# Four of sixteen low parts of a recurrence turn made by GpSimd instead of VectorE

## The chip, the cores and the metric

The program runs on one core of a Trainium2 chip (trn2). Its time is that of one launch on the device, in microseconds, from the first instruction to the last. The median of three runs of the kernel before is given, and one execution of it was profiled.

## The reference

Two layers of a hybrid block and one block of a second kind, for 256 tokens of width 2048 in float32. The part that matters here is the gated delta rule of each layer: 16 heads of width 128, chunks of 64 tokens.

```python
u = h @ w_in
qkv_a, beta_a, a_a, z_a, ... = split_cols(u, SPLIT_SIZES)
qkv_a = jax.nn.silu(causal_conv(qkv_a, conv_w))
q_a, k_a, v_a = ...                      # 16 heads of 128
q_a = l2norm(q_a) * (GDN_HEAD_DIM ** -0.5)
k_a = l2norm(k_a)
o_a = gated_delta_rule(q_a, k_a, v_a, g, beta)
...
# gated_delta_rule: l_mat = strict(k_beta @ k.T * decay), a_mat = l_mat + I
sol = lax.linalg.triangular_solve(a_mat, rhs, lower=True, unit_diagonal=True)
# per chunk: v_new = u - w @ state; o = q @ state + qk @ v_new
#            state = state * dec + k.T @ v_new
```

## The kernel before

**Products in three parts.** All weights and activations are float32, and each is used as a high part, rounded to the format `fp32r`, and a low part, the remainder. A product is high by high, high by low and low by high (L283, L284, L285 in `pe_half`). The weights stream from memory in slabs of 128 x 2048 into a ring of four, `raw`. A slab holds two half blocks of 128 x 1024. For each half block ScalarE makes the high part `Wh` by a copy (`act_cast`, L348), VectorE makes the low part `Wl = raw - Wh` (`dve_low`, L354), and TensorE then has 24 matmuls of 256 columns. `Wh` and `Wl` are rings of four half blocks, so the two engines work three to four half blocks ahead. Counters carry this: `landed` (a slab is in), `hi_ready`, `lo_ready`, `half_used` (TensorE is done with a half block). TensorE waits for `lo_ready` before a half block, and the queue that refills `raw` (SyncE) waits for `lo_ready` too.

**The recurrence loop.** For each layer the 16 heads are taken as 8 pairs. A turn has 16 half blocks (q, k, v and z of one pair of heads, 8 blocks of 128 columns). The first turn of a layer only projects (`fresh`), the last only computes the recurrence of the pair before (`chain`), and the seven turns between do both: they are the full turns, 14 in the program, in a hardware loop. Each engine has its own function for a turn: `pe_gdn`, `act_gdn`, `pool_gdn`, `dve_gdn`. In the last one, half block by half block, n = 0 to 15, stands what VectorE does: `before(n)`, the low part, `after(n)`, `front(n)`. The order on each engine is that of the code. In a full turn VectorE is one late: in step n it makes low part m = n - 1, and the last one after the loop. Low part m of a turn is for half block m + 4; cast m is ScalarE's copy for the same half block, and waits until TensorE has finished half block m.

**What stands around the low parts.** With `LEVEL = 2` and `SCAN = 8`, steps 2 to 7 invert the unit triangular matrix by levels: TensorE makes `Z`, VectorE masks it into `Zm` (L1324), TensorE makes `MZ` (L1104), VectorE writes it into `M` (L1355, `copy_predicated` from PSUM) and packs the next `t_of` by a reduce (L1359). In step 7 VectorE copies `Zm64` out of PSUM (L1316) and TensorE, in the middle of its half block 7, waits for it at L1109. Steps 8 to 12 are the scan over chunks. Beside it, `front` and the table `TAPS` spread the convolution of the next pair over the steps: each channel block has one `tensor_scalar` (L1306, tap 0) and three `scalar_tensor_tensor` (L1309, taps 1 to 3), all 128x256 from SBUF. In step 6 stand tap 3 of one block and taps 0 and 1 of the next, right before `Zm64`. In step 10 stand `vn` (L1333, from PSUM), low 9, the silu product of q and k (L1402, after ScalarE's tanh L1207) and taps 0 and 1 of block 4; in step 11 low 10 and taps 2 and 3; in step 12 the two `sq_lo` (L1428), the low parts of the squares of q and k. TensorE sums these squares with `ones_r` (L1131, L1132, called `ssq`) in its half block 12, after six of its eight tiles.

**GpSimd** makes the three decay matrices of the next pair: `e0`, `e1`, `e2` (L1285, 128x512, rows minus columns) and `E0`, `E1`, `E2` (L1287, plus a mask), with one element pauses (L1257) that carry waits: for the transfer `gb` ahead of `e0`, for TensorE's `Z64` ahead of `e1`, for `turn64` ahead of `odd` (L1281, which clears half of `Mm`), and for `o_second` (L1055) ahead of `e2`.

Of the kernel before, what the change touches and what calls it, by code (L numbers as in the profile page):

```python
# [18 lines left out]
F32 = mybir.dt.float32  # L19
F32R = mybir.dt.float32r  # L20
I32 = mybir.dt.int32
ALU = mybir.AluOpType
# [4 lines left out]
D = 2048  # L27
# [4 lines left out]
PAIRS = HEADS // 2  # L32
# [11 lines left out]
Q_PRE, Q_GDN, Q_END, Q_SWA, Q_OUT = 1, 2 * PAIRS, 8, 2 * KV, 4  # L44
Q_LAYER = Q_PRE + Q_GDN + Q_END + Q_SWA + Q_END + Q_OUT
# [78 lines left out]
def build_program(nc, places, x_t, c_t, pos, stream, ada, ple_w, ple_x, rg_w, rpb, consts, params, params2, out_t, until=None):  # L124
    ctx = ExitStack()
    with ctx:
        def sb(name, shape, dt=F32):
            return ctx.enter_context(nc.sbuf_tensor(name, shape, dt))

        def sem(name):  # L130
            return ctx.enter_context(nc.semaphore(name))
# [6 lines left out]
        raw = sb("raw", [P, 4, D])  # L138
        Wh = sb("Wh", [P, 4, D // 2], F32R)
        Wl = sb("Wl", [P, 4, D // 2], F32R)  # L140
# [20 lines left out]
        def const(name, a=0, b=None):  # L161
            at, n = CONST_AT[name]
            return C[:, at + a:at + (n if b is None else b)]
# [23 lines left out]
        raw_used = sem("raw_used")  # L187
        hi_ready = sem("hi_ready")
        lo_ready = sem("lo_ready")
        half_used = sem("half_used")  # L190
        tile_ready = sem("tile_ready")
        tile_taken = sem("tile_taken")
# [7 lines left out]
        def stage(name, seeded=()):  # L200
            stages.append(Steps(nc, ctx, name, places, seeded))
            return stages[-1]
# [16 lines left out]
        st_gdn = stage("gdn", seeded=("dve",))  # L219
        st_fr = stage("gdn_front")  # L220
# [129 lines left out]
        def dve_low(dve, q, sbk, k):  # L350

            n = 2 * sbk + 4 + k
            dve.wait_ge(hi_ready, q * 8 + n + 1)
            dve.tensor_tensor(Wl[:, n % 4, :], raw[:, (sbk + 2) % 4, k * (D // 2):(k + 1) * (D // 2)],  # L354
                              Wh[:, n % 4, :].bitcast(F32), ALU.subtract).then_inc(lo_ready, 1)

        def act_tile(act, q, sbk):

            act.wait_ge(half_used, q * 8 + (2 * sbk + 2))
# [623 lines left out]
        def u4(v):  # L983
            return v.rearrange("p (u c) -> p u c", u=4)

        def tok(a, c, half=None):

            if half is not None:
                return TOK[:, a, :].rearrange("p (c h t) -> p c h t", h=2, t=2)[:, bass.ds(c, 1), :, half].rearrange("p c h -> p (c h)").unsqueeze(2).to_broadcast([P, 2, P])
            return TOK[:, a, bass.ds(c * 4, 4)].unsqueeze(2).to_broadcast([P, 4, P])  # L990

        def mask4(name):
            return const(name).unsqueeze(1).to_broadcast([P, 4, P])
# [8 lines left out]
        def even(v, odd=0):  # L1002
            return v.rearrange("p u (n two) -> p u n two", two=2)[:, :, :, odd]
# [250 lines left out]
        def pool_gdn(pool, l, i, fresh, chain):  # L1254

            def pause(at=0):
                pool.tensor_tensor(SEC_X[0:1, at:at + 1], ident[0:1, 0:1], ident[0:1, 0:1], ALU.subtract)  # L1257

            S, F = st_gdn, st_fr
            if chain:  # L1260
                S.start("pool")
                r = l * PAIRS + (i - 1)
            if fresh:
                F.start("pool")
                f = l * PAIRS + i
                if not chain:
                    st_pre.wait(pool, "act", "tok_exp", l)
                    pool.tensor_tensor(Zz[:], mask4("ident"), mask4("ident"), ALU.subtract).then_inc(zz_clear, 1)
                F.wait(pool, "dma", "gb", f)
                pause()  # L1270
                rows = [gb[:, 0].rearrange("p h (t c) -> p (h t) c", c=P), gb[:, 1].rearrange("p h (t c) -> p (h t) c", c=P)]
                e = [u4(E[:, n, :]) for n in range(3)]
                for n, (a, b, m) in enumerate(((rows[0], tok(1, i), "m_low"), (tok(0, i), rows[1], "m_up"), (tok(0, i), rows[0], "m_upd"))):
                    if chain and n == 1:
                        S.wait(pool, "pe", "Z64", r)
                        pause()
                    if n == 2:
                        if chain:
                            S.wait(pool, "pe", "turn64", r)
                            pause(8)  # L1280
                        F.done(pool.tensor_tensor(even(Mm[:], 1), even(mask4("ident"), 1), even(mask4("ident"), 1), ALU.mult), "pool", "odd")  # L1281
                    if chain and n == 2:
                        S.wait(pool, "pe", "o_second", r)
                        pause()
                    F.done(pool.tensor_tensor(e[n], a, b, ALU.subtract), "pool", f"e{n}")  # L1285
                    F.wait(pool, "pool", f"e{n}", f)
                    F.done(pool.tensor_tensor(e[n], e[n], mask4(m), ALU.add), "pool", f"E{n}")  # L1287

        def dve_gdn(dve, l, i, fresh, chain):
            S, F, q = st_gdn, st_fr, l * Q_LAYER + Q_PRE + 2 * i  # L1290
# [21 lines left out]
            def before(n):  # L1312
                if n == LEVEL + LEVELS - 1:
                    S.wait(dve, "pe", "Z64", r)
                    dve.wait_ge(zz_clear, l + 1)
                    S.done(dve.tensor_copy(Zz[64:P, :, 0:64], B[0][64:P, 0:256].rearrange("p (u s) -> p u s", u=4)), "dve", "Zm64")  # L1316
                elif LEVEL <= n < LEVEL + PACKED:
                    s = 2 << (n - LEVEL)
                    S.wait(dve, "pe", f"Z{s}", r)
                    if s == 32:  # L1320
                        S.done(dve.tensor_tensor(Zq.rearrange("p (u c) -> p u c", u=4), B[0][:, 0:T].rearrange("p (u c) -> p u c", u=4),
                                                 of_unit.unsqueeze(2).to_broadcast([P, 4, 64]), ALU.mult), "dve", "Zm32")
                        return
                    S.done(dve.tensor_tensor(Zq.rearrange("p (u i c) -> p u i c", u=4, i=4), B[0][:, 0:T].rearrange("p (u i c) -> p u i c", u=4, i=4),  # L1324
                                             sib(n).rearrange("p (u c) -> p u c", u=4).unsqueeze(2).to_broadcast([P, 4, 4, 16]), ALU.mult), "dve", f"Zm{s}")
                if n == SCAN:
                    S.wait(dve, "pe", "WT", r)
                    S.done(dve.tensor_copy(WT[:], B[1][:, 0:2 * P].rearrange("p (h c) -> p h c", c=P)), "dve", "WT")
                if n == SCAN + 2:
                    S.wait(dve, "pe", "VS", r)  # L1330
                    S.wait(dve, "act", "U", r)
                    uu = U[:].rearrange("p (h t) c -> p h t c", t=2)[:, :, 1, :]
                    S.done(dve.tensor_tensor(uu, uu, B[2][:, 0:2 * P].rearrange("p (h c) -> p h c", c=P), ALU.subtract), "dve", "vn")  # L1333
# [84 lines left out]
            for n in range(16):  # L1418
                if chain:
                    before(n)  # L1420

                if fresh and n == (SCAN + 4 if chain else SCAN + 3):
                    for h in range(2):
                        if not chain:
                            F.done(dve.memset(SEC_X[0:1, 16 + h:17 + h], 0.0), "dve", f"sq_lo{h}")
                            continue
                        F.wait(dve, "act", f"sq{h}", f)
                        F.done(dve.tensor_tensor(sq_lo[h], tm2[:, 2 * h:2 * h + 2, :], sq_hi[h].bitcast(F32), ALU.subtract), "dve", f"sq_lo{h}")  # L1428
                if n or not chain:
                    late = 1 if chain else 0  # L1430
                    dve_low(dve, q + (n - late) // 8, (n - late) // 2 % 4, (n - late) % 2)
                if chain:
                    after(n)
                if fresh:
                    front(n)
# [1446 lines left out]
def build(scratch, nc, shapes, until=None):  # L2882

    places = {}
    for core in (scratch, nc):
        args = [core.dram_tensor(f"in_{n}", shape, dt, kind="ExternalInput").ap() for n, (shape, dt) in shapes.items()]
        args.append(core.dram_tensor("out_0", (P, KT, T), F32, kind="ExternalOutput").ap())
        build_program(core, places, *args, until=until)
# [12 lines left out]
```

## Time and profile before

| | |
|---|---|
| median of three runs | 3900.39 us (3900.19 to 3901.93) |
| span of the profiled execution | 3899.3 us |
| TensorE busy | 3753.7 us, 96% |
| VectorE busy | 2862.0 us, 73% |
| ScalarE busy | 1904.5 us, 49% |
| GpSimd busy | 186.2 us, 5% |
| low parts (L354) | 1124, mean 1235 ns |
| casts (L348) | 1124, mean 1047 ns |
| share of the chain that ended last | PE 83%, DVE 8%, ACT 4% |

In the profile PE is TensorE's matmuls, DVE VectorE, ACT ScalarE, POOL GpSimd. A busy share says which engine has little air, and the list of waits says whether another engine ever keeps it waiting. Matmuls are pipelined: one is shown as 0.28 us long, but the next starts 0.12 us later. A duration of VectorE or GpSimd is counted from its issue, so that the time in which it is held up by the other is inside it: two rows of the same line and shape with different durations are the thing to look for.

### The profile page before, as it was taken

What the parts mean: (1) busy time and instruction counts of PE and PEld (TensorE: products, weight loads), DVE (VectorE), ACT (ScalarE), POOL (GpSimd) and SP (SyncE); (2) the same over time, 40 slices, a digit from 0 to 9 for tenths busy, and PEclk for the clock granted to TensorE, in tenths of its full rate; (3) what the DMA queues carried; (4) which work ended last, traced back from release to release, by engine and by line L of the source; (5) the groups of instructions that cost most, each with busy time, mean ns of one, the idle gap of its engine ahead of it and who ended that gap; (6) DMA issues with size and microseconds to landing.
All of it is one profiled execution on the core that took longest, in us unless ns stands there. A gap on an engine that the chain in (4) does not pass through costs nothing.

```text
span 3899.3 us, 70287 instructions
## 1 busy us (share of the span) xinstructions
PE 3753.7 (96%) x27254; PEld 3506.0 (90%) x27254; DVE 2862.0 (73%) x3924; ACT 1904.5 (49%) x2898; POOL 186.2 (5%) x188
## 2 busy tenths in 40 slices
PE   1999999999999999999999999999999999999998
PEld 1999999899988999999989998999987888989888
DVE  8788887867779778888686776665676666666676
ACT  1556565335544355555534554454665433334365
POOL 0111111000000012121000000000000000000000
PEclk8999999999999999999999999999999999999999
DMA  9543443864468843434486444444534455555543
GB/s 397 180 146 139 143 141 139 305 228 166 152 242 315 284 147 141 149 136 151 143 316 216 158 153 178 182 164 174 189 121 150 173 184 184 184 184 184 182 143 129
DMA packets 138699, 720.49 MB, mean 185 GB/s; under 512 B 37696, under 2 KB 38144, under 8 KB 62336
## 3 DMA queue, kind: packets, MB, share of 16 engines
q1 hardware_dynamic: 111456, 631.31, 45.1%
q10 hardware_dynamic: 27040, 86.32, 6.5%
q8 instruction: 146, 2.39, 0.2%
q14 instruction: 57, 0.47, 0.0%
HBM read 711.22 MB, written 2.16 MB: 183 GB/s over the span
## 4 chain that ended last, share of the span: by engine, by line
PE 83%; DVE 8%; ACT 4%; issue 3%; DMA 2%; DVEq 0%; ACTq 0%; SPq 0%
PE bank L300 16%; PE bank L283 13%; PE bank L285 13%; PE bank L284 13%; PE bank L301 8%; PE bank L322 3%; PE bank L2408 2%; PE bank L2410 2%; PE bank L2409 2%; ACT Wh L348 2%; PE bank L326 2%; DMA raw<-in_ada 1%; DVE Wl L354 1%; PE bank L1075 1%; DVE gm_more L1306 1%
## 5 line engine op out<-in xcount | busy, mean ns | idle before, releaser
L348 ACT CAST Wh<-raw 128x1024 fp32r<-128x1024 f32 x1124 | 1167.5, 1047 | 1617.8 <-PE bank L285 917.4
L354 DVE TENSOR_TENSOR Wl<-raw,Wh 128x1024 fp32r<-128x1024 f32 x1124 | 1380.9, 1235 | 701.4 <-ACT Wh L348 698.4
L283 PE MATMUL bank<-H,Wh 128*128 128x256 f32 x4928 | 1446.6, 294 | 2.0 <-DVE Wl L354 1.2
L284 PE MATMUL bank<-H,Wh 128*128 128x256 f32 x4928 | 1393.8, 283 | 0.0
L285 PE MATMUL bank<-H,Wl 128*128 128x256 f32 x4928 | 1393.1, 283 | 0.0
L283 PEld LDWEIGHTS bank<-H,Wh 128*128 128x128 f32 x4928 | 942.4, 191 | 26.1 <-issue 13.6
L284 PEld LDWEIGHTS bank<-H,Wh 128*128 128x128 f32 x4928 | 943.0, 191 | 8.1 <-issue 4.8
L285 PEld LDWEIGHTS bank<-H,Wl 128*128 128x128 f32 x4928 | 942.0, 191 | 0.0
L300 PE MATMUL bank<-H,Wh 128*128 128x512 f32 x1792 | 632.8, 397 | 6.3 <-DVE WS L341 6.2
L301 PE MATMUL bank<-H,Wl 128*128 128x256 f32 x1792 | 502.3, 280 | 0.0
L300 PEld LDWEIGHTS bank<-H,Wh 128*128 128x128 f32 x1792 | 337.4, 188 | 90.2 <-DVE Wl L354 5.3
L301 PEld LDWEIGHTS bank<-H,Wl 128*128 128x128 f32 x1792 | 339.3, 189 | 0.0
L300 PE MATMUL bank<-O,Wh 128*128 128x512 f32 x896 | 321.6, 401 | 6.2 <-DVE both L341 6.2
L301 PE MATMUL bank<-O,Wl 128*128 128x256 f32 x896 | 252.5, 282 | 0.0
L300 PEld LDWEIGHTS bank<-O,Wh 128*128 128x128 f32 x896 | 170.0, 190 | 50.8 <-DVE Wl L354 6.5
L2408 PE MATMUL bank<-O,Wh 128*128 128x256 f32 x704 | 199.9, 284 | 2.8 <-DVE WS L341 2.8
L2409 PE MATMUL bank<-O,Wh 128*128 128x256 f32 x704 | 199.1, 283 | 0.0
L2410 PE MATMUL bank<-O,Wl 128*128 128x256 f32 x704 | 199.1, 283 | 0.0
L301 PEld LDWEIGHTS bank<-O,Wl 128*128 128x128 f32 x896 | 170.9, 191 | 0.0
L326 PE MATMUL bank<-H,Wl 128*128 128x256 f32 x576 | 162.0, 281 | 0.0
L322 PE MATMUL bank<-H,Wh 128*128 128x512 f32 x384 | 139.2, 404 | 7.3 <-DVE H L602 2.8
L2408 PEld LDWEIGHTS bank<-O,Wh 128*128 128x128 f32 x704 | 134.9, 192 | 5.0 <-issue 4.5
(417 smaller groups left out, 4498.8 us busy)
## 6 DMA issues: line engine op xcount, KB each, us to landing
raw<-in_stream SPq DMA_DIRECT2D x560, 1024.0 KB, 4.8
WS<-in_ada ACTq DMA_DIRECT2D x94, 512.0 KB, 6.3
raw<-in_ada SPq DMA_DIRECT2D x32, 1024.0 KB, 7.5
gm_more<-in_ada ACTq DMA_DIRECT2D x20, 512.0 KB, 6.7
WS<-rows_d ACTq DMA_DIRECT2D x16, 512.0 KB, 5.0
KR<-in_ada ACTq DMA_DIRECT2D x14, 512.0 KB, 6.6
raw<-in_stream SPq DMA_DIRECT2D x8, 512.0 KB, 7.0
gm_more<-WS ACTq DMA_DIRECT2D x32, 128.0 KB, 4.7
```

Of the source, the lines that this page charges most:

```text
L283: pe.matmul(out[:, 0:T], wh, xh[:, kt, :], start=first, stop=False)
L284: pe.matmul(out[:, 0:T], wh, xl[:, kt, :], start=False, stop=False)
L285: mm = pe.matmul(out[:, 0:T], wl, xh[:, kt, :], start=False, stop=last)
L300: pe.matmul(out[:, :], wh, x[:, kt, :, :], start=kt == 0, stop=False)
L301: mm = pe.matmul(out[:, 0:T], wl, x[:, kt, 0, :], start=False, stop=kt == KT - 1)
L322: pe.matmul(out[:, :], wh, x[:, kt, :, :], start=first, stop=False)
L326: mm = pe.matmul(out[:, 0:T], wl, x[:, kt, 0, :], start=False, stop=last)
L348: act.copy(Wh[:, n % 4, :], raw[:, (sbk + 2) % 4, k * (D // 2):(k + 1) * (D // 2)]).then_inc(hi_ready, 1)
L354: dve.tensor_tensor(Wl[:, n % 4, :], raw[:, (sbk + 2) % 4, k * (D // 2):(k + 1) * (D // 2)], Wh[:, n % 4, :].bitcast(F32), ALU.subtract).t ...
L2408: pe.matmul(o, wh, ah, start=x == 0, stop=False)
L2409: pe.matmul(o, wh, al, start=False, stop=False)
L2410: m = pe.matmul(o, wl, ah, start=False, stop=x == 3)
```

## The change

GpSimd gets `pool_low`, the same subtraction as `dve_low`, for m = 1, 5, 9 and 13 of a full turn. It counts up its own counter `low_by_pool`. VectorE leaves these four out. With the low part that follows each (m = 2, 6, 10, 14) it first waits for `low_by_pool` and then adds 2 to `lo_ready` (`dve_low_two`). On GpSimd low 1 and low 5 stand at the start of the turn ahead of the wait for `gb`, low 9 after `E1` and ahead of the pause for `turn64`, low 13 at the end. First and last turns of a layer stay as they are.

```diff
--- before.py
+++ after.py
@@ -187,6 +187,7 @@
         raw_used = sem("raw_used")
         hi_ready = sem("hi_ready")
         lo_ready = sem("lo_ready")
+        low_by_pool = sem("low_by_pool")
         half_used = sem("half_used")
         tile_ready = sem("tile_ready")
         tile_taken = sem("tile_taken")
@@ -353,6 +354,23 @@
             dve.wait_ge(hi_ready, q * 8 + n + 1)
             dve.tensor_tensor(Wl[:, n % 4, :], raw[:, (sbk + 2) % 4, k * (D // 2):(k + 1) * (D // 2)],
                               Wh[:, n % 4, :].bitcast(F32), ALU.subtract).then_inc(lo_ready, 1)
+
+        LOW_ON_POOL = (1, 5, 9, 13)
+
+        def pool_low(pool, q, sbk, k):
+
+            n = 2 * sbk + 4 + k
+            pool.wait_ge(hi_ready, q * 8 + n + 1)
+            pool.tensor_tensor(Wl[:, n % 4, :], raw[:, (sbk + 2) % 4, k * (D // 2):(k + 1) * (D // 2)],
+                               Wh[:, n % 4, :].bitcast(F32), ALU.subtract).then_inc(low_by_pool, 1)
+
+        def dve_low_two(dve, q, sbk, k, pooled):
+
+            n = 2 * sbk + 4 + k
+            dve.wait_ge(low_by_pool, pooled)
+            dve.wait_ge(hi_ready, q * 8 + n + 1)
+            dve.tensor_tensor(Wl[:, n % 4, :], raw[:, (sbk + 2) % 4, k * (D // 2):(k + 1) * (D // 2)],
+                              Wh[:, n % 4, :].bitcast(F32), ALU.subtract).then_inc(lo_ready, 2)
 
         def act_tile(act, q, sbk):
 
@@ -1256,7 +1274,12 @@
             def pause(at=0):
                 pool.tensor_tensor(SEC_X[0:1, at:at + 1], ident[0:1, 0:1], ident[0:1, 0:1], ALU.subtract)
 
-            S, F = st_gdn, st_fr
+            S, F, q = st_gdn, st_fr, l * Q_LAYER + Q_PRE + 2 * i
+
+            def low(n):
+                if fresh and chain:
+                    pool_low(pool, q + n // 8, n // 2 % 4, n % 2)
+
             if chain:
                 S.start("pool")
                 r = l * PAIRS + (i - 1)
@@ -1266,6 +1289,8 @@
                 if not chain:
                     st_pre.wait(pool, "act", "tok_exp", l)
                     pool.tensor_tensor(Zz[:], mask4("ident"), mask4("ident"), ALU.subtract).then_inc(zz_clear, 1)
+                low(1)
+                low(5)
                 F.wait(pool, "dma", "gb", f)
                 pause()
                 rows = [gb[:, 0].rearrange("p h (t c) -> p (h t) c", c=P), gb[:, 1].rearrange("p h (t c) -> p (h t) c", c=P)]
@@ -1275,6 +1300,7 @@
                         S.wait(pool, "pe", "Z64", r)
                         pause()
                     if n == 2:
+                        low(9)
                         if chain:
                             S.wait(pool, "pe", "turn64", r)
                             pause(8)
@@ -1285,6 +1311,7 @@
                     F.done(pool.tensor_tensor(e[n], a, b, ALU.subtract), "pool", f"e{n}")
                     F.wait(pool, "pool", f"e{n}", f)
                     F.done(pool.tensor_tensor(e[n], e[n], mask4(m), ALU.add), "pool", f"E{n}")
+                low(13)
 
         def dve_gdn(dve, l, i, fresh, chain):
             S, F, q = st_gdn, st_fr, l * Q_LAYER + Q_PRE + 2 * i
@@ -1426,9 +1453,12 @@
                             continue
                         F.wait(dve, "act", f"sq{h}", f)
                         F.done(dve.tensor_tensor(sq_lo[h], tm2[:, 2 * h:2 * h + 2, :], sq_hi[h].bitcast(F32), ALU.subtract), "dve", f"sq_lo{h}")
-                if n or not chain:
-                    late = 1 if chain else 0
-                    dve_low(dve, q + (n - late) // 8, (n - late) // 2 % 4, (n - late) % 2)
+                late = 1 if chain else 0
+                m = n - late
+                if fresh and chain and m - 1 in LOW_ON_POOL:
+                    dve_low_two(dve, q + m // 8, m // 2 % 4, m % 2, (l * (PAIRS - 1) + (i - 1)) * 4 + (m // 4 + 1))
+                elif m >= 0 and not (fresh and chain and m in LOW_ON_POOL):
+                    dve_low(dve, q + m // 8, m // 2 % 4, m % 2)
                 if chain:
                     after(n)
                 if fresh:
```

The order on GpSimd at the start of a full turn, before (L1257 is the pause for `gb`, L1285 is `e0`, L1287 is `E0`):

```order
L2666 ISA
L1257 TENSOR_TENSOR SEC_X<-C 1x1 [waits gdn_front_dma_done]
L1285 ISA
L1285 TENSOR_TENSOR WS<-WS,TOK 128x512
L121 ISA
L1287 TENSOR_TENSOR WS<-WS,C 128x512 [waits gdn_front_pool_done]
```

And now; the lines have moved by some 20 (L1275 is the pause, L1311 `e0`, L364 the new subtraction):

```order
L2696 ISA
L364 TENSOR_TENSOR Wl<-raw,Wh 128x1024 [waits hi_ready]
L363 REGISTER_ALU
L364 TENSOR_TENSOR Wl<-raw,Wh 128x1024 [waits hi_ready]
L121 ISA
L1275 TENSOR_TENSOR SEC_X<-C 1x1 [waits gdn_front_dma_done]
L1311 ISA
L1311 TENSOR_TENSOR WS<-WS,TOK 128x512
L121 ISA
L1313 TENSOR_TENSOR WS<-WS,C 128x512 [waits gdn_front_pool_done]
```

Low 1 and low 5 stand ahead of the pause and `e0`.

GpSimd from `E1` to `e2` of a full turn, before (L1281 is `odd`; the pause ahead of it waits for `turn64`, the one behind it for `o_second`):

```order
L1287 TENSOR_TENSOR WS<-WS,C 128x512 [waits gdn_front_pool_done]
L121 REGISTER_ALU
L1257 TENSOR_TENSOR SEC_X<-C 1x1 [waits gdn_pe_done]
L1281 TENSOR_TENSOR WS<-C 128x256
L121 REGISTER_ALU
L1257 TENSOR_TENSOR SEC_X<-C 1x1 [waits gdn_pe_done]
L1285 TENSOR_TENSOR WS<-TOK,WS 128x512
```

And now (L1313 is `E1`, L1307 is `odd`):

```order
L1313 TENSOR_TENSOR WS<-WS,C 128x512 [waits gdn_front_pool_done]
L363 ISA
L364 TENSOR_TENSOR Wl<-raw,Wh 128x1024 [waits hi_ready]
L121 REGISTER_ALU
L1275 TENSOR_TENSOR SEC_X<-C 1x1 [waits gdn_pe_done]
L1307 TENSOR_TENSOR WS<-C 128x256
L121 REGISTER_ALU
L1275 TENSOR_TENSOR SEC_X<-C 1x1 [waits gdn_pe_done]
L1311 TENSOR_TENSOR WS<-TOK,WS 128x512
```

Low 9, which waits for cast 9, stands between `E1` and `odd`; `odd` and `e2` are behind it in the queue.

VectorE in steps 10 and 11, behind `vn`, before (L354 is low 9 and then low 10, L1402 the silu product, L1306 and L1309 taps 0 and 1):

```order
L353 REGISTER_ALU
L354 TENSOR_TENSOR Wl<-raw,Wh 128x1024 [waits hi_ready]
L121 ISA
L1402 SCALAR_TENSOR_TENSOR gm_more<-gm_more 128x1024 [waits gdn_front_act_done]
L1302 REGISTER_ALU
L1306 ISA [waits tile_taken]
L1306 TENSOR_SCALAR Y<-Y,PAR 128x256
L121 REGISTER_ALU
L1309 ISA [waits gdn_front_dve_done]
L1309 SCALAR_TENSOR_TENSOR Y<-Y,PAR 128x256
L353 REGISTER_ALU
L354 TENSOR_TENSOR Wl<-raw,Wh 128x1024 [waits hi_ready]
```

And now, behind `vn` (L1429 is the silu product, L1333 and L1336 the taps, L372 low 10 with its report of two):

```order
L121 ISA
L1429 SCALAR_TENSOR_TENSOR gm_more<-gm_more 128x1024 [waits gdn_front_act_done]
L1329 REGISTER_ALU
L1333 ISA [waits tile_taken]
L1333 TENSOR_SCALAR Y<-Y,PAR 128x256
L121 REGISTER_ALU
L1336 ISA [waits gdn_front_dve_done]
L1336 SCALAR_TENSOR_TENSOR Y<-Y,PAR 128x256
L370 REGISTER_ALU
L371 REGISTER_ALU [waits low_by_pool]
L372 TENSOR_TENSOR Wl<-raw,Wh 128x1024 [waits hi_ready]
```

Low 9 is gone ahead of the silu product, and low 10 has a wait for `low_by_pool` ahead of it.

## Rows read from the trace of the kernel before

**Rows 1.** Busy time by engine, one full turn: span, then PE, PEld, DVE, ACT, POOL

```profile
203.90:266.40 62.50, 61.94 (x492) 59.68 (x491) 53.29 (x84) 36.04 (x57) 10.23 (x11) 1.00 0.40 142
```

**Rows 2.** TensorE's waits over the whole span: total us, times, longest

```profile
PE bank L1109 <- DVE WS L1316: 4.1, 14, 0.6
```

**Rows 3.** Timeline of VectorE, steps 10 to 12: start us, duration us

```profile
295.68 1.22 DVE L354 TENSOR_TENSOR Wl<-raw,Wh 128x1024 fp32r<-128x1024 f32 x1
296.87 1.23 DVE L1402 SCALAR_TENSOR_TENSOR gm_more<-gm_more 128x1024 f32<-128x1024 f32 x1
298.01 1.28 DVE L1306 TENSOR_SCALAR Y<-Y,PAR 128x256 f32<-128x256 f32 x1
299.43 1.33 DVE L1309 SCALAR_TENSOR_TENSOR Y<-Y,PAR 128x256 f32<-128x256 f32 x1
300.69 1.21 DVE L354 TENSOR_TENSOR Wl<-raw,Wh 128x1024 fp32r<-128x1024 f32 x1
...
302.85 1.29 DVE L1428 TENSOR_TENSOR O<-gm_more,O 128x512 fp32r<-128x512 f32 x2
```

**Rows 4.** Timeline of TensorE at `ssq` in the same turn

```profile
304.59 0.39 PE L1131 MATMUL bank<-O,ones_r 128*128 128x512 f32 x1
```

**Rows 5.** Timeline of GpSimd in the same stretch

```profile
297.06 1.08 POOL L1257 TENSOR_TENSOR SEC_X<-C 1x1 f32<-1x1 f32 x1 [11.23 <-PE bank L1055]
298.10 1.03 POOL L1285 TENSOR_TENSOR WS<-TOK,WS 128x512 f32<-128x512 f32 x1
299.21 1.28 POOL L1287 TENSOR_TENSOR WS<-WS,C 128x512 f32<-128x512 f32 x1
```

**Rows 6.** Timeline of VectorE, steps 6 and 7 of the turn before

```profile
215.14 1.23 DVE L354 TENSOR_TENSOR Wl<-raw,Wh 128x1024 fp32r<-128x1024 f32 x1 [0.23 <-ACT Wh L348]
216.47 0.46 DVE L1355 COPY_PREDICATED WS<-C,bank 128x256 f32<-128x256 int32 x1
...
217.16 0.53 DVE L1309 SCALAR_TENSOR_TENSOR gm_more<-Y,PAR,gm_more 128x256 f32<-128x256 f32 x1 [0.23 <-DVE WS L1355]
217.62 1.36 DVE L1306 TENSOR_SCALAR gm_more<-Y,PAR 128x256 f32<-128x256 f32 x1
219.12 1.18 DVE L1309 SCALAR_TENSOR_TENSOR gm_more<-Y,PAR,gm_more 128x256 f32<-128x256 f32 x1
220.33 0.43 DVE L1316 COPY WS<-bank 64x256 f32<-64x256 f32 x1
```

**Rows 7.** Timeline of GpSimd in that stretch

```profile
216.37 1.03 POOL L1285 TENSOR_TENSOR WS<-WS,TOK 128x512 f32<-128x512 f32 x1
...
218.98 1.03 POOL L1285 TENSOR_TENSOR WS<-TOK,WS 128x512 f32<-128x512 f32 x1
...
222.52 0.60 POOL L1281 TENSOR_TENSOR WS<-C 128x256 f32<-128x256 f32 x1
```

**Rows 8.** GpSimd's largest subtractions, late in the program: duration ns min/median/max

```profile
L2673 POOL TENSOR_TENSOR Y<-C x4: 1896/2385/2879, 3009.1 to 3015.6; 128x1024 f32<-128x1024 f32 x4
```

**Rows 9.** Timeline of VectorE at low 13, low 14, then low 1

```profile
312.38 1.22 DVE L354 TENSOR_TENSOR Wl<-raw,Wh 128x1024 fp32r<-128x1024 f32 x1 [1.72 <-ACT Wh L348]
...
316.04 1.23 DVE L354 TENSOR_TENSOR Wl<-raw,Wh 128x1024 fp32r<-128x1024 f32 x1 [1.30 <-ACT Wh L348]
...
324.58 1.23 DVE L354 TENSOR_TENSOR Wl<-raw,Wh 128x1024 fp32r<-128x1024 f32 x1 [0.20 <-ACT Wh L348]
...
326.70 0.63 DVE L1359 TENSOR_REDUCE WS<-WS 128x64 f32<-128x256 f32 x1
```

**Rows 10.** Timeline of TensorE, first matmul of the half block of low 13

```profile
319.99 0.28 PE L283 MATMUL bank<-H,Wh 128*128 128x256 f32 x1
```

**Rows 11.** Timeline of ScalarE at cast 9: idle time before it, and tanh

```profile
294.56 1.05 ACT L348 CAST Wh<-raw 128x1024 fp32r<-128x1024 f32 x1 [2.27 <-PE bank L285]
...
295.77 1.06 ACT L1207 ACTIVATE gm_more<-gm_more 128x1024 f32<-128x1024 f32 x1
```

**Rows 12.** Timeline of TensorE at L1109 in the turn of rows 6

```profile
220.81 1.10 PE L1109 MATMUL bank<-WS 128*128 128x64 f32 x8 [0.25 <-DVE WS L1316]
```

## Prediction

> **What bounds the kernel now.** I read first the busy times of one full turn of the recurrence loop [rows 1]: the turn takes 62.5 us, TensorE is busy 61.9 of them at the full clock (2.4 GHz), VectorE 53.3, GpSimd 10.2. So TensorE sets the pace, and VectorE counts only where TensorE waits for it. The list of TensorE's waits says where that is: fourteen times, once a turn, L1109 waits for `Zm64` (L1316), 4.1 us in all or 0.29 a turn [rows 2]. Nothing in a full turn waits for a low part (`Wl`). The most that relief of VectorE can bring is therefore near 4 us of 3900, and a delay of VectorE costs as soon as it reaches a place where TensorE has no slack. I then read the four timelines around the block with the least slack, `ssq` (L1131): VectorE delivers `sq_lo1` at 302.85 + 1.29 = 304.14 [rows 3], and TensorE takes it at 304.59 [rows 4]. The slack is 0.45 us. Half block numbers n below are TensorE's within a turn; "low m" is the subtraction that makes the half block m + 4; a "cast" is ScalarE's part of it.
>
> **What runs on the two engines at the same time.** The timelines show that GpSimd and VectorE exclude each other for most of these forms. At 298.01 a 128x256 tensor_scalar takes 1.28 us and ends 0.16 after GpSimd's `e2` (298.10 + 1.03 = 299.13); at 299.43 the next tap takes 1.33 and ends 0.27 after `E2` (300.49) [rows 3, 5]. The reverse too: GpSimd's 1x1 pause takes 1.08 us, until VectorE's silu (L1402) ends at 298.10 [rows 3, 5]. Operations with a PSUM source are free of it: `M64` (L1355) runs inside `e0` in 0.46 us [rows 6, 7]. The first question is thus not how much VectorE saves, but what it wants to do while GpSimd subtracts.
>
> **What the change takes off and puts on.** VectorE loses 4 subtractions a turn, 1.22 us each [rows 3, 6]: 4.9 us a turn, 56 of them in 14 full turns. GpSimd gets them. Their form, 128x1024 with two full inputs, is not in the trace. Lower bound: the 128x1024 subtraction of a constant from itself, 1.90 at its fastest [rows 8]. Upper bound: twice the 128x512 addition of a mask, 2 x 1.28 = 2.56 [rows 5]. I take 2.4: the same twice, less the fixed part paid once (2 x 1.03 of `e2` less 1.90 = 0.16), since that form too reads two different arrays. The Trainium skill, page "GPSIMD Engine Reference", section 3.1, gives 4497 ns for 2048 fp32 elements, half of which is 2.25; by that figure, an estimate, both terms below shrink by 0.15 a turn and the time would be 3919. No row here shows it.
>
> **Low 1 and low 13: nothing.** Low 1 starts about 324.6, where low 1 stood [rows 9], and ends at 327.0. VectorE has there `M4` with a PSUM source and a one-input reduce at 326.70. `M4` waits for TensorE's product and not for the low part ahead of it, so its start does not move. If the reduce were shut out too, it would lose 0.3; I take 0. Low 13 runs from 312.4, where it stood [rows 9], to 314.8. VectorE has nothing to do there but silu's product `qkn`, which now comes before it because low 13 no longer stands ahead; it then waits for cast 14 until 316.04 [rows 9]. The report of a moved block comes with the next low. The next cast comes one half block later, 62.5 / 16 = 3.9 us, which is more than 2.4, so the new wait of VectorE is over before the old one. The tightest report is low 13's: with low 14 it is out at 316.04 + 1.23 = 317.27, and TensorE starts that half block at 319.99 [rows 9, 10], 2.7 us later. The refill of `raw` is released by the same count and leaves one half block later; ScalarE waits in the turn for TensorE and not for that transfer (at cast 9, 2.27 us for L285 [rows 11]), so 0.
>
> **Low 5: +0.30 us a turn.** It starts at 215.14 [rows 6] and ends at 217.54. Tap 3 (issued 217.16) now waits for that instead of for `e0` (217.40) and ends 0.29 after it, 217.83. The queued pause and `e0` come in ahead of the tensor_scalar, as pause and `e2` did at 298.10: 218.86. Tensor_scalar 0.16 later, 219.02. `E0` 1.28, 220.30. The next tap ends 0.29 behind, 220.60, where today it ends at 219.12 + 1.18 = 220.30 behind `e1` [rows 6, 7]. One GpSimd operation has slipped in at the front, one (`e1`) has slipped out at the back, and the new one is longer. `Zm64` starts 0.30 later, and L1109, which already waits for it [rows 12], waits 0.30 more.
>
> **Low 9: +1.35 us a turn.** Cast 9 ends at 294.56 + 1.05 = 295.61 [rows 11]. VectorE's own low 9 started at 295.68 and was free of cost, since silu could not start before tanh ended at 296.83 [rows 3, 11]. GpSimd now holds from 295.66 to 298.06. Silu waits: it ends at 299.2 and not at 298.1. And GpSimd's queue has been kept behind low 9: the pause and `odd` (0.60 [rows 7]), which ran at 222.5, now run here, right after silu: 299.8. Tensor_scalar: 299.96. Pause and `e2`: 301.0. Tap: 301.3. `E2`: 302.55. Low 10: 303.65. From the end of low 10 to the end of `sq_lo1` today it is 304.14 - 301.90 = 2.24 [rows 3]: 305.9. TensorE wanted it at 304.59 [rows 4] and starts about 305.95. That is 1.35 us of standing still for an engine that has no other work, because its instructions go in order. Nothing gives it back: TensorE has no idle time later in the turn to use up.
>
> **The sum.** 14 x (0.30 + 1.35) = 23.1 us. The profiled execution spans 3899.3 us, the median is 3900.39; the difference of 1.1 is outside the change and stays. Forecast: 3900.4 + 23.1 = 3923 us, +0.6%. About 0.2% (7.8 us) is what a measurement of this kernel can tell from no change.
>
> **The rivals.**
> *VectorE gets the ties, or the subtraction is short: about 3910.* I let GpSimd's queued operation go first where both wait. If VectorE does, at low 5 the tensor_scalar goes at 218.0, `e0` after it, `Zm64` at 219.35, and the 0.29 of L1109 is gone; at low 9 the operations sort differently but most of them still stand ahead of `sq_lo`, 305.5 by the same steps, 0.95 late. Sum 14 x 0.66 = 9 us: 3910. The subtraction at its lower bound of 1.90 takes 0.5 off the low 9 term and 0.4 off the other: 14 x 0.75 = 10.5 us: 3911. For it: both are within the rows. Against it: tensor_scalar was issued at 298.01, ahead of `e2` at 298.10, and lost [rows 3, 5]. The Trainium skill, page "SBUF — State Buffer", section "SBUF: two separate sides", says that whichever starts first gets the shared pair for the whole instruction; by that rule the tensor_scalar would have won, and this rival is what the rule would give. The trace disagrees in this one place, and agrees that the loser waits for the whole instruction.
> *The cover holds: about 3896.* If a two-input VectorE operation isn't shut out by this subtraction, VectorE is 1.2 us ahead at `Zm64` and L1109's wait goes: 14 x 0.29 = 4 us gained, within 0.2%. It decides from the point at which silu can start at 296.87. Faster than 3892.6 would need other waits to go as well, of which VectorE is not the cause. Against it stand four stretched rows [rows 3, 6].
> *GpSimd is slower than its bounds: about 3937.* Rows of GpSimd at 128x1024 reach 2.88 [rows 8], though with VectorE in the way. At 2.9, 0.5 more at each of the two places: 14 x 1.0 = 14 us more.
> *The change doesn't do what it says:* if low 13 took over 3.6 us (312.4 to 316.04), VectorE would wait for GpSimd, and the blocks would come late. The bounds speak against it.
>
> **How the numbers follow.** Forecast 0.55; cheaper (3910) 0.2; cover holds 0.1; slower GpSimd 0.12; 0.03 for what I don't see. The range takes in the forecast, the cheaper case and most of the dearer: 3906 to 3938. It leaves out the cover case and tails, some 0.18. Faster by over 0.2% (under 3892.6): 0.03. Within 0.2%: the cover case and the low edge of the cheaper one, 0.13. Slower: 0.84.
>
> **What would show it.** In the profile after: the GpSimd subtraction at about 2.4 us, 56 times; silu (now L1429) stretched to about 2.3 us from an issue soon after tanh; a new wait of TensorE at `ssq` for VectorE's `sq_lo`, 14 times, 1.2 to 1.4 us; L1109's wait grown from 0.29 to about 0.6; a full turn of about 64.1 us; no wait for `Wl` and none of VectorE for `low_by_pool`. Wrong would be: `ssq` without a wait (then silu was not held), L1109's wait shorter (then VectorE won the ties), or a time outside the fourteen turns that moved.

## The result and the profile after

The changed kernel takes 3920.26 us, median of five runs (3919.83 to 3922.09), beside 3900.39 for the kernel before in the same session. The ratio of the two, estimated over all runs, is 1.0057, with a 95% interval of 1.0046 to 1.0068, or 18 to 27 us: slower, by 19.9 us between the medians. The forecast was 3923, range 3906 to 3938. Of all executions of the kernels below, one (earlier taps, with low 1 and 13 on GpSimd) fell in a slow state, 7222.33 us at a granted clock of 0.95 where the others show 0.99, and it is left out of that kernel's median.

The profiled execution spans 3918.0 us. First the busy times of one full turn, from one copy of `Zm64` to the next (span, then PE, PEld, DVE, ACT, POOL), to be held against [rows 1]:

```profile
220.88:284.88 64.00, 62.37 (x491) 59.89 (x491) 51.12 (x79) 36.15 (x57) 19.92 (x17) 1.00 0.39 140
```

VectorE's busy time is 2 us less (its four low parts are gone, but what is left is held longer), GpSimd's about 10 us more, and the turn is 1.5 us longer. The clock is the full one in both. So the engine that was relieved was not the one that sets the pace, and moving its work made the turn longer.

TensorE's waits, from the matmuls' side (total us, times, longest), against [rows 2]:

```profile
PE bank L1149 <- DVE O L1455: 13.9, 14, 1.0
PE bank L1127 <- DVE WS L1343: 7.1, 14, 0.5
...
PE bank L1137 <- ACT WS L1206: 3.3, 16, 0.3
```

L1137 (L1119 before) is as long as before, 3.3 us. L1149 is `ssq` (L1131 before): a wait that was not there at all now stands once in each of the 14 full turns. L1127 is the wait for `Zm64` (L1109 before), up from 4.1 to 7.1. The same two waits from the side of the weight load, which stands idle a little earlier than the matmul behind it, measure the lost time better:

```profile
PEld bank L1149 <- DVE O L1455: 16.7, 14, 1.2
...
PEld bank L1127 <- DVE WS L1343: 10.0, 14, 0.7
```

The second was this before the change:

```profile
PEld bank L1109 <- DVE WS L1316: 6.9, 14, 0.8
```

16.7 plus 10.0 - 6.9 = 3.1 makes 19.8 us, close to the 19.9 between the medians. That the match is this close is partly chance, since the interval is 18 to 27 us. The turns of the same two profiled executions say it independently: from the first to the seventh `Zm64` a turn of the first layer grew by 1.42 us (62.58 to 64.00) and one of the second by 1.50, 20.4 us over the fourteen. VectorE never waits for `low_by_pool`: its only waits at L372 are for the cast (14 times).

GpSimd's subtraction, whose duration nothing before the change showed (ns, min/median/max), against the 1896 of [rows 8]:

```profile
L364 POOL TENSOR_TENSOR Wl<-raw,Wh x56: 2371/2394/2412, 199.7 to 1902.6; 128x1024 fp32r<-128x1024 f32 x56
```

**Low 9, in the second full turn.** VectorE in steps 10 to 12, against [rows 3]:

```profile
298.72 2.28 DVE L1429 SCALAR_TENSOR_TENSOR gm_more<-gm_more 128x1024 f32<-128x1024 f32 x1 [1.10 <-ACT gm_more L1225]
300.93 0.84 DVE L1333 TENSOR_SCALAR Y<-Y,PAR 128x256 f32<-128x256 f32 x1
301.92 1.18 DVE L1336 SCALAR_TENSOR_TENSOR Y<-Y,PAR 128x256 f32<-128x256 f32 x1
303.01 2.32 DVE L372 TENSOR_TENSOR Wl<-raw,Wh 128x1024 fp32r<-128x1024 f32 x1
...
306.28 1.28 DVE L1455 TENSOR_TENSOR O<-gm_more,O 128x512 fp32r<-128x512 f32 x2
```

GpSimd in the same stretch, against [rows 5]:

```profile
297.54 2.38 POOL L364 TENSOR_TENSOR Wl<-raw,Wh 128x1024 fp32r<-128x1024 f32 x1 [9.42 <-ACT Wh L349]
299.88 1.17 POOL L1275 TENSOR_TENSOR SEC_X<-C 1x1 f32<-1x1 f32 x1
301.01 0.60 POOL L1307 TENSOR_TENSOR WS<-C 128x256 f32<-128x256 f32 x1
301.58 0.23 POOL L1275 TENSOR_TENSOR SEC_X<-C 1x1 f32<-1x1 f32 x1
301.77 1.03 POOL L1311 TENSOR_TENSOR WS<-TOK,WS 128x512 f32<-128x512 f32 x1
302.88 1.36 POOL L1313 TENSOR_TENSOR WS<-WS,C 128x512 f32<-128x512 f32 x1
```

And TensorE at `ssq`, against [rows 4]:

```profile
307.62 0.50 PE L1149 MATMUL bank<-O,ones_r 128*128 128x512 f32 x1 [1.02 <-DVE O L1455]
```

The three timelines are to be read as one. VectorE is idle for 1.10 us ahead of silu, so the removed low part left a hole that nothing could use, since silu waits for the tanh (L1225). Silu is issued at 298.72 and lasts 2.28 us instead of 1.23, because GpSimd holds until 299.92. `odd` (301.01 to 301.61) goes in ahead of the tensor_scalar, which was issued at 300.93 and ends at 301.77, 0.16 behind it. `e2` ends at 302.80 and the tap at 303.10. `E2` ends at 304.24 and low 10, issued at 303.01, at 305.33. `sq_lo1` ends at 307.56, and TensorE, idle for 1.02 us, starts at 307.62.

**Low 5, in the first full turn.** VectorE up to `Zm64`, against [rows 6]:

```profile
217.45 0.71 DVE L1336 SCALAR_TENSOR_TENSOR gm_more<-Y,PAR,gm_more 128x256 f32<-128x256 f32 x1 [0.23 <-DVE WS L1382]
218.08 1.27 DVE L1333 TENSOR_SCALAR gm_more<-Y,PAR 128x256 f32<-128x256 f32 x1
219.50 1.35 DVE L1336 SCALAR_TENSOR_TENSOR gm_more<-Y,PAR,gm_more 128x256 f32<-128x256 f32 x1
220.88 0.43 DVE L1343 COPY WS<-bank 64x256 f32<-64x256 f32 x1
```

GpSimd beside it, against [rows 7]:

```profile
215.48 2.39 POOL L364 TENSOR_TENSOR Wl<-raw,Wh 128x1024 fp32r<-128x1024 f32 x1 [13.37 <-ACT Wh L349]
217.84 0.36 POOL L1275 TENSOR_TENSOR SEC_X<-C 1x1 f32<-1x1 f32 x1
218.17 1.03 POOL L1311 TENSOR_TENSOR WS<-WS,TOK 128x512 f32<-128x512 f32 x1
219.28 1.29 POOL L1313 TENSOR_TENSOR WS<-WS,C 128x512 f32<-128x512 f32 x1
```

Each of the three tap operations ends 0.15 to 0.3 us behind one operation of GpSimd: behind low 5, `e0` and `E0`, where it was `e0`, `E0` and `e1` before. All of this turn lies 0.30 later by an offset from ahead of it; of the 0.55 by which `Zm64` is later, 0.25 is the change's.

### The profile page after: what moved, and what is told of

Same layout as the page of the kernel before. It is cut to its first block, busy times and chain, and to the rows that moved or that the text cites. A ratio compares the mean times of both kernels' runs of the same rounds, so it can differ in the third digit from the quotient of the medians.

```text
span 3918.0 us, 70399 instructions
## 1 busy us (share of the span) xinstructions
PE 3752.9 (96%) x27254; PEld 3506.7 (90%) x27254; DVE 2826.9 (72%) x3868; ACT 1906.1 (49%) x2898; POOL 321.4 (8%) x244
## 4 chain that ended last, share of the span: by engine, by line
PE 78%; DVE 9%; issue 7%; ACT 4%; DMA 2%; DVEq 0%; ACTq 0%; SPq 0%
PE bank L301 15%; PE bank L284 12%; PE bank L285 12%; PE bank L286 12%; PE bank L302 8%; PE bank L323 3%; PE bank L2438 2%; PE bank L2440 2%; PE bank L2439 2%; PE bank L327 2%; ACT Wh L349 2%; DMA raw<-in_ada 1%; DVE Wl L355 1%; DVE WS L1382 1%; PE bank L1093 1%
## 5 line engine op out<-in xcount | busy, mean ns | idle before, releaser
L355 DVE TENSOR_TENSOR Wl<-raw,Wh 128x1024 fp32r<-128x1024 f32 x1012 | 1237.2, 1229 | 652.6 <-ACT Wh L349 650.9
L301 PEld LDWEIGHTS bank<-O,Wh 128*128 128x128 f32 x896 | 169.7, 189 | 49.7 <-DVE Wl L355 7.0
L364 POOL TENSOR_TENSOR Wl<-raw,Wh 128x1024 fp32r<-128x1024 f32 x56 | 133.9, 2391 | 658.9 <-ACT Wh L349 658.9
```

What stands on the lines that cost most here:

```text
L301: pe.matmul(out[:, :], wh, x[:, kt, :, :], start=kt == 0, stop=False)
```

## The experiments

The theory (A): the whole cost is VectorE shut out while GpSimd subtracts, in two places, low 5 and low 9, and in the second place the work that low 9 held back on GpSimd adds to it. The rival (B): each moved part costs by itself, through the added wait and the late report. All these kernels are `after` with one edit unless it is said otherwise. Their ratios to the kernel before carry an interval of 0.1 to 0.17% to either side, or 4 to 7 us, so the length of a full turn stands beside them: the copies of `Zm64` in the seven full turns of the second layer, last start less first start, over six. The rows are those of `Zm64` (ns min/median/max, first and last start in us), of the kernel before and of the change:

```profile
L1316 DVE COPY WS<-bank x7: 427/428/428, 1475.6 to 1850.7; 64x256 f32<-64x256 f32 x7
```

```profile
L1343 DVE COPY WS<-bank x7: 427/427/428, 1487.9 to 1872.0; 64x256 f32<-64x256 f32 x7
```

375.1 / 6 = 62.52 and 384.1 / 6 = 64.02 us.

**Low 1 and low 13 alone.**

```diff
-        LOW_ON_POOL = (1, 5, 9, 13)
+        LOW_ON_POOL = (1, 13)
...
-                if fresh and chain:
+                if fresh and chain and n in LOW_ON_POOL:
                     pool_low(pool, q + n // 8, n // 2 % 4, n % 2)
```

The running count that VectorE waits for is adapted. In the next two the tuple is `(5,)` and `(9,)`.

> Only low 1 and low 13 are made by GpSimd, low 5 and low 9 by VectorE as before. Theory A (what costs is VectorE being shut out while GpSimd subtracts, at low 5 and low 9): VectorE has nothing with two SBUF inputs to do in these two places, so 3900 us, within 2 of before, no wait of TensorE at ssq, L1109's wait 0.25 to 0.3 a turn. Rival B (each moved part costs by itself, through VectorE's added wait and the late report of two): half of the 20 us, 3910.

Measured: 3901.25 beside 3901.61, ratio 1.0000 (0.9991 to 1.0010). The turn:

```profile
L1343 DVE COPY WS<-bank x7: 427/427/428, 1475.4 to 1850.4; 64x256 f32<-64x256 f32 x7
```

375.0 / 6 = 62.50. There is no wait at `ssq`; L1127 waits 4.0 us in 14 times. Rival B, which wanted 3910, is out: 28 parts moved, with wait and double report, cost nothing that can be measured. They bring nothing either.

**Low 5 alone.**

> Only low 5 is made by GpSimd. Theory A: L1109's wait grows from 0.25 to 0.51 us a turn and nothing else, 14 x 0.26 = 3.6 us, so 3904. Rival B (a price for each moved part): a quarter of 20 us, 3905, but without a longer wait at L1109.

Measured: 3903.97, ratio 1.0004 (0.9994 to 1.0014). The wait at `Zm64`, in this kernel:

```profile
PE bank L1127 <- DVE WS L1343: 7.2, 14, 0.5
```

It is the 7.1 of the full change, and `ssq` has none. In the second layer the turn is 62.88 us beside 62.52, in the first 62.77 (376.6 / 6) beside 62.58. The time alone would not tell it from no change; the wait does.

**Low 9 alone.**

> Only low 9 is made by GpSimd. Theory A: the wait at ssq of about 1.0 us (1.28 of lost time) a turn is there in full, 14 x 1.28 = 17.9 us, so 3918, and L1109's wait is 0.25. Rival B: a quarter of 20 us, 3905.

Measured: 3918.58, ratio 1.0047 (1.0030 to 1.0063). The waits and the turn:

```profile
PE bank L1149 <- DVE O L1455: 14.0, 14, 1.0
...
PE bank L1127 <- DVE WS L1343: 3.8, 14, 0.5
```

```profile
L1343 DVE COPY WS<-bank x7: 427/428/428, 1476.5 to 1858.9; 64x256 f32<-64x256 f32 x7
```

382.4 / 6 = 63.73, 1.21 more than before. One moved part of four makes the whole wait at `ssq`.

**`odd` ahead of low 9.** All four moved, one line of GpSimd's order changed:

```diff
                     if n == 2:
-                        low(9)
                         if chain:
                             S.wait(pool, "pe", "turn64", r)
                             pause(8)
                         F.done(pool.tensor_tensor(even(Mm[:], 1), ...), "pool", "odd")
+                        low(9)
```

> All four moved as in the change, but GpSimd does odd and its pause ahead of low 9 instead of behind it. Theory A with its second part (0.60 us of the ssq term is odd, which low 9 had held back until VectorE had no air): ssq loses 0.6 less a turn, 14 x 0.6 = 8.4 us, so 3912, silu still 2.28 us long. If the place of odd doesn't matter (only low 9 itself does): 3920.

Measured: 3915.13, ratio 1.0033 (1.0019 to 1.0047). The waits:

```profile
PE bank L1127 <- DVE WS L1343: 7.1, 14, 0.5
PE bank L1149 <- DVE O L1455: 6.8, 14, 0.5
```

`ssq` waits 6.8 instead of 13.9 us, 0.51 a turn less, and the turn is 63.5 instead of 64.0. Silu is as long as in the change (2.28), so it is the displaced `odd` that is gone from VectorE's way. About 0.5 of the 1.2 us belongs to it.

**The late report alone.** VectorE makes all low parts; 1, 5, 9 and 13 don't count up, the next one counts two, and GpSimd and the wait for it are left out:

```diff
+                elif fresh and chain and m in LOW_ON_POOL:
+                    dve_low_silent(dve, q + m // 8, m // 2 % 4, m % 2)
```

> VectorE makes all low parts itself, but 1, 5, 9 and 13 report nothing, and the next one reports two, as in the change; GpSimd gets no subtraction. Theory A: the late report has 2.7 us or more to spare at each place and the refill of raw is early enough, so 3900, no new wait of TensorE. Rival B (the late report costs): L1149 or the half blocks wait for Wl, 3905 or more.

Measured: 3900.03 beside 3900.24, ratio 0.9998 (0.9989 to 1.0007), a turn of (1847.8 - 1472.8) / 6 = 62.50, no new wait. The report one half block later, and with it the later refill of `raw`, is free.

**Low 9 in two instructions.**

```diff
-            pool.tensor_tensor(Wl[:, n % 4, :], raw[...], Wh[:, n % 4, :].bitcast(F32), ALU.subtract)
+            for a, b in ((0, 512), (512, 1024)):
+                x = pool.tensor_tensor(Wl[:, n % 4, a:b], raw[...], Wh[:, n % 4, a:b].bitcast(F32), ALU.subtract)
```

Only low 9 is split; the other three stay whole, and the report goes with the last part.

> As the change, but GpSimd makes low 9 in two instructions of 128x512. Theory A counts the work that must pass one after the other between cast 9 and sq_lo, not the length of an instruction: silu starts after the first part and is no longer stretched much (under 1.6 us), the second part goes behind it and shuts out the tensor_scalar instead; with 0.15 us more for a second start, ssq waits 1.0 to 1.2 us and the time is 3920 to 3923. Rival C (only a silu held for long costs): ssq's wait falls by a half or more, 3911.

Measured: 3920.15, ratio 1.0057 (1.0042 to 1.0071). GpSimd's two parts in one row (1.28 us, then 2.32 from issue to end), then VectorE beside them:

```profile
297.42 3.56 POOL L366 TENSOR_TENSOR Wl<-raw,Wh 128x512 fp32r<-128x512 f32 x2 [9.41 <-ACT Wh L349]
```

```profile
298.59 1.23 DVE L1432 SCALAR_TENSOR_TENSOR gm_more<-gm_more 128x1024 f32<-128x1024 f32 x1 [1.10 <-ACT gm_more L1228]
299.74 1.39 DVE L1336 TENSOR_SCALAR Y<-Y,PAR 128x256 f32<-128x256 f32 x1
```

```profile
PE bank L1152 <- DVE O L1458: 13.8, 14, 1.0
```

Silu has its 1.23 us back, and nothing is won: the second part stands behind silu and pushes the tensor_scalar, and `ssq` waits 13.8 us as with one instruction (13.9). What counts is the sum of what must pass one after the other between cast 9 and `sq_lo`. Rival C, that a long held silu is the harm, is out.

**Memsets in place of low 9.** Low 9 alone is moved, and GpSimd fills the same tile, and the used half of `raw`, with zeros. The kernel leaves out the low part of that half block. The 1x1 subtraction ahead of the memsets only carries the wait:

```diff
-            pool.tensor_tensor(Wl[:, n % 4, :], raw[...], Wh[...].bitcast(F32), ALU.subtract).then_inc(low_by_pool, 1)
+            pool.tensor_tensor(SEC_X[0:1, 12:13], ident[0:1, 0:1], ident[0:1, 0:1], ALU.subtract)
+            pool.memset(Wl[:, n % 4, :].bitcast(F32), 0.0)
+            x = pool.memset(raw[...], 0.0)
+            x.then_inc(low_by_pool, 1)
```

> Only low 9 is moved, and instead of the subtraction GpSimd fills Wl and the used half of raw with zeros: two memsets, no tensor read (this leaves the low part of that half block out of the result). If it is reading from SBUF on both sides that excludes, silu keeps its 1.23 us though GpSimd is busy beside it, and ssq waits only for the displaced odd, 0.2 us a turn, about 3903. If any work of GpSimd shuts VectorE out, silu is stretched until the memsets end and ssq waits 0.6 or more, 3909 or more.

Measured: 3903.34 in one run. GpSimd, then VectorE:

```profile
295.64 0.94 POOL L365 MEMSET Wl<- 128x1024 f32 x1
296.53 0.95 POOL L366 MEMSET raw<- 128x1024 f32 x1
297.45 0.52 POOL L1277 TENSOR_TENSOR SEC_X<-C 1x1 f32<-1x1 f32 x1
```

```profile
296.70 1.23 DVE L1431 SCALAR_TENSOR_TENSOR gm_more<-gm_more 128x1024 f32<-128x1024 f32 x1 [1.10 <-ACT gm_more L1227]
```

Silu starts 0.17 us into the second memset and takes 1.23 us as if it were alone, in all 14 full turns (1225 to 1227 ns). A 1x1 subtraction of GpSimd issued meanwhile waits until silu ends. So it is not GpSimd's being busy or its writing that shuts VectorE's two-input operation out; what the memsets lack is the reading from SBUF. That they differ in nothing else that matters isn't shown. The turn is (1852.7 - 1476.7) / 6 = 62.67, 0.15 over before. That fits the displaced `odd` (0.60, at 297.93 right behind silu) less the slack of 0.45 at `ssq`: no wait is listed there, but in the turn shown the weight load of `ssq` starts at 304.51, 0.19 later than its pace of 0.12 us would have it.

**Earlier taps, with low 1 and low 13 on GpSimd.** The reading of [rows 6] says what makes `Zm64` late in the kernel before: three taps that take turns with GpSimd. `after` with low 1 and 13, and the taps of block 0 spread from step 2 on, so that step 6 has two tap operations and not three:

```diff
-        TAPS = {4: ((0, (0, 1)),), 5: ((0, (2,)),), 6: ((0, (3,)), (1, (0, 1))), ...
+        TAPS = {2: ((0, (0,)),), 4: ((0, (1, 2)),), 5: ((0, (3,)),), 6: ((1, (0, 1)),), ...
```

> Low 1 and low 13 on GpSimd as in e1, and the taps of the convolution start earlier: tap 0 of block 0 in step 2, where low 1 left 1.2 us, taps 1 and 2 in step 4, tap 3 in step 5, so that step 6 has two taps and not three ahead of Zm64. Theory A (VectorE's part of the wait at L1109 is the taps that take turns with e0, E0, e1): Zm64 comes 1.2 us earlier, the wait of 0.25 to 0.29 a turn is gone, 14 x 0.27 = 3.8 us, so 3896.5 against 3900.4. Rival: TensorE then waits for something else (t_of at L1093), 3900 or more.

Measured: 3893.88, median of eleven, beside 3900.24, ratio 0.9985 (0.9976 to 0.9994). The wait at `Zm64` is gone from the list.

**Earlier taps alone**, in the kernel before, with the one before beside it once more:

> The kernel before with the earlier taps of e9 and nothing on GpSimd. If e9's gain is the order of the taps alone, this has it too: no wait at L1109 for Zm64, 3895. If the 1.2 us that low 1 leaves in step 2 is needed for tap 0, low 2 is late here and TensorE waits longer at L1075 for t_of, 3898 or more.

> The kernel of e9 once more, beside e8 on the same chip: 0.9985 of the kernel before. Within 0.05% of e8 if the moved low parts bring nothing of their own.

Measured: 3891.15 for the taps alone and 3890.23 with low 1 and 13 on GpSimd, beside 3899.53; ratios 0.9980 (0.9971 to 0.9988) and 0.9978 (0.9969 to 0.9988). VectorE up to `Zm64` with the taps alone:

```profile
279.35 0.40 DVE L1306 TENSOR_SCALAR gm_more<-Y,PAR 128x256 f32<-128x256 f32 x1 [0.23 <-DVE WS L1355]
279.89 1.34 DVE L1309 SCALAR_TENSOR_TENSOR gm_more<-Y,PAR,gm_more 128x256 f32<-128x256 f32 x1
281.27 0.43 DVE L1316 COPY WS<-bank 64x256 f32<-64x256 f32 x1
```

```profile
282.59 1.00 PE L1109 MATMUL bank<-WS 128*128 128x64 f32 x8
```

`Zm64` is ready at 281.70 and TensorE takes it at 282.59, 0.9 us later, without a wait. The turn is (1845.6 - 1472.8) / 6 = 62.13, and 62.02 in the first layer. So this kernel is faster than the one before and than the change, though VectorE still makes every low part of 1.2 us: one short tap fewer in step 6 is enough. Low 1 and 13 on GpSimd add nothing to it that can be measured.

## Why the prediction was right

**The bound.** "A delay of VectorE costs as soon as it reaches a place where TensorE has no slack": the new wait stands at `ssq`, where the slack was 0.45 us. What relief could bring was put at 4 us from the matmuls' idle time of 0.29 a turn. That term was too small: with that wait gone by earlier taps, a turn became 0.56 us shorter in the first layer and 0.39 in the second, 6.6 us in 14, and the median fell by 8.4 (with an interval of some 3.5 to either side). The weight load's idle time before the change, 6.9 us, would have been the better bound.

**The subtraction.** 2.4 taken between 1.90 and 2.56; measured 2.394. The row of the mask addition, with two different inputs, was the right neighbour and the row of the constant the wrong one. The figure of the Trainium skill, page "GPSIMD Engine Reference", section 3.1, halved to an estimate of 2.25, was 0.14 too short for this form.

**Low 1 and low 13: nothing.** Right, by the run with these two alone. The reduce, taken at 0 where it might have lost 0.3, starts at 329.82 in the profile after, while low 1 runs from 327.74 to 330.14, and takes 0.62 us, no longer than before. The late report and the later refill were rightly put at nothing too, by the run with the report alone.

**Low 5: +0.30.** The mechanism was right down to the order of the operations: low 5, tap 3, `e0`, tensor_scalar, `E0`, tap. The size was 0.22 by the weight load's waits (3.1 / 14) and 0.25 by `Zm64`. GpSimd's `E0` as I took it, 1.28 after the tensor_scalar's end, was too long: it is issued at 219.28, and 0.07 of its 1.29 us lie ahead of that end (219.35).

**Low 9: +1.35.** The size was 1.19 (16.7 / 14) over all turns; in the turn shown, the first matmul behind `ssq` starts 1.27 late (308.65 for 305.52, less 1.86). Taken back by the 1.86 us by which TensorE is already late in this turn, the steps forecast and measured are: silu's end 299.2 and 299.14, `odd` 299.8 and 299.75, `e2` 301.0 and 300.94, `E2` 302.55 and 302.38, low 10 303.65 and 303.47, `sq_lo1` 305.9 and 305.70. Again `E2` is the term that was too long. That the displaced `odd` is part of it is confirmed by the run with `odd` ahead: 0.51 us, where its 0.60 was counted.

**The sum.** 3.1 + 16.7 = 19.8 us in place of 23.1, against 19.9 between the medians. No two errors made up for each other: both terms were too large, by 1.1 and 2.2 us. The interval of the time alone, 18 to 27 us, would have allowed 23.1 as well; it is the waits that show the terms too large.

**The rivals.** VectorE getting the ties was wrong: behind silu, the tensor_scalar issued at 300.93 let `odd`, issued at 301.01, go first, and behind tap 3 the one issued at 218.08 let `e0`, issued at 218.17. The reason given, that GpSimd's queued operation goes first where both wait, is wider than the rows. In both places, and at 298.01 before the change, GpSimd's operation stood right behind a one element pause that had been waiting for VectorE since before the tensor_scalar was issued (299.88, 217.84, 297.06). At the other meetings in these rows the one issued earlier goes first, of either engine: tap 3 (217.45) ahead of the pause (217.84) behind low 5, `E2` (302.88) ahead of low 10 (303.01). The Trainium skill, page "SBUF — State Buffer", section "SBUF: two separate sides", has the one that starts first win; read as the order of issue, it agrees with these rows except for the operation right behind such a pause. What makes that exception was not tried. The same section says that two SBUF inputs conflict only with a GpSimd operation that reads SBUF; the run with the memsets agrees with it. That the cover holds, and that GpSimd is slower than its bounds, did not come about.

**Left open.** The spans of the two profiled executions differ by 18.7 us where the two waits make 19.8. Outside the recurrence, where the program is the same, the distance between the same cast of ScalarE in the two executions jumps by up to 1.6 us, in both directions. What makes it jump was not tried. These jumps are why turns were compared beside medians.

## What to carry to other kernels

In this kernel, work moved from VectorE to GpSimd (here a subtraction of two tensors in SBUF) shuts VectorE out for its longer duration wherever VectorE has one of the operations to do that are held here (silu, the taps); where it has none, as at low 1 and low 13, the move is free. Ask what VectorE wants to do in those microseconds, and what stands behind the moved operation in GpSimd's own queue. And look first at the place where the pacing engine waits: here three short tap operations stood ahead of the awaited copy, and with one of them fewer the kernel gained 8.4 us, where moving four large operations a turn cost 19.9.

## What the runs showed of the hardware

GpSimd's memset of 128x1024 (0.94 us) and a two-input VectorE operation (1.23 us) ran side by side, neither longer than alone, while a 1x1 subtraction of GpSimd waited for VectorE's operation to end. Where the two engines held each other up, the operation issued first went first, except that one of GpSimd right behind a waiting pause went ahead of one of VectorE issued 0.08 or 0.09 us earlier. A wait of TensorE is longer by the weight load's count than by the matmul's (1.2 against 1.0 at `ssq`, 0.49 against 0.29 a turn at `Zm64` before), and the former is what the time followed: with low 9 alone the weight load waits 1.20 us a turn (16.8 / 14) and the turn is 1.17 and 1.21 longer in the two layers; with the 0.49 gone, it is 0.56 and 0.39 shorter.
